# First projection of a two-block transformer kernel: its weights in quarters, x's second tile between them

## The reference

```
hn = rms_norm(h, attn_norm)
z = hn @ w_in                       # 1024 x 2048: q, k, v and u, 512 columns each
a_out = diff_attention(q, k, v, positions, q_norm, k_norm, lam_*, subln)
p_out = pool_mixer(u, w_pool, pool_scale)
h = h + concat(a_out, p_out) @ w_out
h = h + moe(rms_norm(h, ffn_norm), ...)     # 32 experts, each token in 4
```

## Time and profile before

| | us |
|---|---|
| median of 3 runs | 1755.04 (1754.52 to 1757.65) |
| profiled execution, its own time | 1755.88 |
| its span | 1753.7 |
| TensorE busy | 1677.8 (96%) |
| VectorE busy | 394.5 (22%) |
| ScalarE busy | 284.8 (16%) |
| HBM read | 654.14 MB, 374 GB/s over the span |

### The profile page before, as it was taken

How to read it: one execution, slowest core, us unless ns; L and a number is a source line. 1 busy time by engine, 2 the same in 40 slices (tenths; PEclk the granted TensorE clock), 3 DMA queues, 4 the chain that set the end, 5 groups by cost and what they waited for, 6 DMA issues and landing times.

```text
span 1753.7 us, 28543 instructions
## 1 busy us (share of the span) xinstructions
PE 1677.8 (96%) x11960; PEld 770.6 (44%) x11960; DVE 394.5 (22%) x943; ACT 284.8 (16%) x559; POOL 44.7 (3%) x115
## 2 busy tenths in 40 slices
PE   8999999999999999999999989999999999988887
PEld 4643333333333333333333334755545665654444
DVE  3543122121122112121121122453331111111111
ACT  3311111111121101100110012130112222111111
POOL 3140000000000000000000000000000000000000
PEclk9999999999999999999999999999999999999999
DMA  9769999999999999999999995533389999999997
GB/s 323 233 234 424 428 429 427 429 429 427 428 427 428 428 428 423 428 428 426 429 429 427 429 408 210 188 109 131 114 321 409 425 429 428 429 429 428 429 429 308
DMA packets 74394, 656.08 MB, mean 374 GB/s; under 512 B 13296, under 2 KB 16128, under 8 KB 36960
## 3 DMA queue, kind: packets, MB, share of 16 engines
q1 hardware_dynamic: 70880, 651.39, 89.7%
q0 software_dynamic: 688, 2.51, 0.4%
q10 hardware_dynamic: 2768, 1.31, 0.3%
HBM read 654.14 MB, written 1.05 MB: 374 GB/s over the span
## 4 chain that ended last, share of the span: by engine, by line
PE 76%; DMA 21%; DVE 1%; ACT 1%; issue 0%; SPq 0%; DVEq 0%
PE ps L1726 32%; DMA ring<-in_w_up_experts 11%; PE ps L1766 8%; PE ps L2132 6%; DMA ring<-in_w_up 6%; PE ps L2072 5%; PE ps L1711 4%; DMA scr<-in_w_up 4%; PE ps L1550 3%; PE ps L1817 3%; PE ps L1795 2%; PE ps L1720 2%; PE ps L1618 2%; PE ps L2310 2%; PE ps L1823 1%; PE ps L1781 1%
## 5 line engine op out<-in xcount | busy, mean ns | idle before, releaser
L1726 PE MATMUL ps<-ring,Z 128*64 128x512 f32 x2304 | 509.0, 595 | 11.9 <-DMA ring<-in_w_up 11.3
L1726 PEld LDWEIGHTS ps<-ring,Z 128*64 128x64 f32 x2304 | 165.5, 137 | 321.4 <-issue 291.4
L1766 PE MATMUL ps<-ring,Z 128*32 128x128 f32 x2752 | 164.8, 409 | 15.0 <-DMA ring<-in_w_up_experts 8.8
L1726 PE MATMUL ps<-scr,Z 128*64 128x512 f32 x768 | 170.3, 594 | 5.7 <-DMA scr<-in_w_up 5.7
L1766 PEld LDWEIGHTS ps<-ring,Z 128*32 128x32 f32 x2752 | 105.5, 127 | 70.4 <-DMA ring<-in_w_up_experts 13.3
L2132 PE MATMUL ps<-ring,both_x 128*128 128x512 f32 (+1 forms) x256 | 105.8, 567 | 0.0
L1726 PEld LDWEIGHTS ps<-scr,Z 128*64 128x64 f32 x768 | 54.8, 137 | 109.2 <-issue 95.2
L1711 PE MATMUL ps<-h,Z 128*32 128x256 f32 (+1 forms) x776 | 99.8, 468 | 0.5 <-DVE Z L1076 0.4
L1106 DVE TENSOR_SCALAR Z<-ps 128x512 f32<-128x512 f32 x32 | 22.1, 691 | 334.1 <-PE ps L1726 334.1
L677 ACT COPY Z<-ps 128x256 f32<-128x256 f32 (+1 forms) x63 | 30.1, 478 | 303.7 <-PE ps L1726 229.7
L668 ACT COPY Z<-ps 128x256 f32<-128x256 f32 x64 | 23.8, 372 | 312.8 <-PE ps L1774 312.8
(11 more groups left out here) (445 smaller groups left out, 1434.5 us busy)
## 6 DMA issues: line engine op xcount, KB each, us to landing
ring<-in_w_gate SPq DMA_DIRECT2D x48, 2048.0 KB, 24.6
ring<-in_w_up SPq DMA_DIRECT2D x48, 2048.0 KB, 27.2
ring<-in_w_down SPq DMA_DIRECT2D x48, 2048.0 KB, 29.4
ring<-in_w_gate_experts SPq DMA_DIRECT2D x21, 2048.0 KB, 32.4
ring<-in_w_up_experts SPq DMA_DIRECT2D x21, 2048.0 KB, 31.8
ring<-in_w_down_experts SPq DMA_DIRECT2D x21, 2048.0 KB, 31.3
scr<-in_w_down SPq DMA_DIRECT2D x16, 2048.0 KB, 28.7
scr<-in_w_gate SPq DMA_DIRECT2D x16, 2048.0 KB, 28.5
```

Of the source, the lines that this page charges most:

```text
L1726: last = pe.matmul(dst[CAP * j:CAP * (j + 1)], lhsT, rhs(j), start=start, stop=True, skip_group_check=True)
L1766: last = pe.matmul(bank(4)[CAP2 * t:CAP2 * (t + 1), P * s:P * (s + 1)], picked[:, chunk * CAP2:(chunk + 1) * CAP2], v[:, c, t:512:4], star ...
```

## The change

The first slot's weights come in four pieces of two chunks instead of two pieces of four. SyncE issues x tile 0, the gain, quarter 0, quarter 1, x tile 1, quarter 2, quarter 3 and then the slots as before. TensorE turns x tile 0, multiplies its first four chunks as the quarters land, turns tile 1, and multiplies the last four; the waits for `norm_xT` and for the weights come every two chunks. The turns fill the same banks in the same order. ScalarE, VectorE and GpSimd keep their code.

```diff
-        FRONT_PIECES = [2] + [1] * (SLOTS - 1)
+        FRONT_PIECES = [4] + [1] * (SLOTS - 1)
@@ SyncE
-            for a in range(TT):
+            def load_x(a):
                 sp.dma_start(h[:, a, :], w["x"][0, a * P:(a + 1) * P, :]).then_inc(sem(f"x_loaded{a}"), 16)
+
+            load_x(0)
             sp.dma_start(gcol[:, A_NORM, :], w["attn_norm"][0].rearrange("(p c) -> p c", p=P)).then_inc(sem("gain_loaded"), 16)
             for s, (src, c, n) in enumerate(front):
                 per = c // FRONT_PIECES[s]
                 for part in range(FRONT_PIECES[s]):
                     r = slice(part * per, (part + 1) * per)
-                    sp.dma_start(slot(s, c, n)[:, r, :], src[:, r, :]).then_inc(sem("first_half") if s == part == 0 else full[s], 16)
+                    sp.dma_start(slot(s, c, n)[:, r, :], src[:, r, :])\
+                        .then_inc(full[s] if part == FRONT_PIECES[s] - 1 else sem(f"first_quarter{part}"), 16)
+                    if s == 0 and part == 1:
+                        load_x(1)
@@ TensorE
-            for b in range(4):
-                pe.wait_ge(sem(f"x_loaded{b // 2}"), 16)
-                turn(bank(4 + b), h[:, b // 2, :], 4 * (b % 2), DC, 4, "norm_turned")
+
+            def turn_x(a):
+                pe.wait_ge(sem(f"x_loaded{a}"), 16)
+                for half in range(2):
+                    turn(bank(4 + 2 * a + half), h[:, a, :], 4 * half, DC, 4, "norm_turned")
 
             def project_in(j):
 
                 u, a = j // 2, j % 2
-                pe.wait_ge(sem("norm_xT"), 2 * a + 2)
-                pe.wait_ge(*((full[u], 16) if j else (sem("first_half"), 16)))
+                if j:
+                    pe.wait_ge(sem("norm_xT"), 2 * a + 2)
+                    pe.wait_ge(full[u], 16)
                 if j >= 2:
                     pe.wait_ge(sem("z_copied"), j - 1)
                 for c in range(DC):
                     if j == 0 and c == DC // 2:
-                        pe.wait_ge(full[0], 16)
+                        turn_x(1)
+                    if j == 0 and c % 2 == 0:
+                        pe.wait_ge(sem("norm_xT"), c // 4 + 1)
+                        pe.wait_ge(sem(f"first_quarter{c // 2}") if c < 6 else full[0], 16)
                     last = pe.matmul(bank(j % 2), xT[:, c, a * P:(a + 1) * P], slot(u, DC, 512)[:, c, :],
                                      start=c == 0, stop=c == DC - 1)
                 last.then_inc(sem("proj"), 1)
 
+            turn_x(0)
             for j in range(6):
                 project_in(j)
```

## The result

The changed kernel takes 1760.15 us (median of 11 runs, 1757.99 to 1765.95) against 1755.54 for the kernel before (11 runs, 1754.52 to 1757.65); the ratio is 1.0028, 95% interval 1.0019 to 1.0036. It is slower, by 4.6 us (0.28%; the interval leaves no change out). The profiled execution took 1759.94 with a span of 1757.8: 4.1 over the one of before.

What follows compares the result with a forecast made beforehand. TensorE was taken to bound the kernel (76% of the chain, DMA 21%). A wait of +3.2 and a slow restart of +1.8 gave +5.0 us, 1760.0 against 1755.04; 8-in-10 range 1755.6 to 1763.6.

Steps and rivals of the forecast that it cites:

- Landings: First slot and x tiles: quarter 0 at 6.2 to 7.5, tile 1 at 8.5 to 10.9, last quarter 13.4 or up to 1 later.
- turn_x(1): TensorE's turns of x tile 1 start at 12.6 us, bounds 10.9 and 13.9, after eight instructions taking 5.6.
- The gain: First projection ends at 16.9 instead of 19.6: 2.7 us saved, bounds 1.4 and 4.4; fourth ends at 37.5.
- The root: ScalarE's root, behind x tile 1's means, comes at 14.7 instead of 8.98: 5.7 us later, bounds 4.4 and 7.0.
- the whole shift passes: The small loads behind the root land later by its whole 5.7 us, `w_pool` at 38.9.
- The slack: In the kernel before, the third copy ends at 37.6, the fifth projection starts at 40.2: 2.6 us to spare.
- The wait: TensorE starts the fifth projection at 43.4 instead of 40.2, +3.2 us, after some 5.9 us idle.
- The restart: TensorE's slow clock after idling ahead of the fifth projection: +1.8 us, bounds 0 and 3.6.
- Nothing absorbs it: Behind the projections and through the expert stage, the shift of +5.0 us reaches the kernel's end whole.

Runs made afterwards that it cites:

- after_again: The changed kernel, unchanged, profiled once more; span 1762.7 us.
- before_again: The kernel before, unchanged, profiled once more; span 1754.6 us.
- kept_busy: The changed kernel with 22 bf16 products of zeros into a free bank ahead of the fifth projection; 1763.36 us, ratio 1.0055 to the kernel before.
- quarters_only: The kernel before with slot 0 in four quarters, both x tiles still in front; 1756.31 us, ratio 1.0000 to the kernel before.
- loads_late: The kernel before with five squares into unused space on ScalarE ahead of the small loads; 1756.14 us, ratio 1.0000.
- held_slots: The changed kernel with SyncE issuing slots 3 to 5 only when the nine small loads have landed; 1752.17 us, ratio 0.9977 to the kernel before.
- loads_early: The changed kernel with the small loads issued between the squares of the two x tiles; 1756.92 us, ratio 1.0006 to the kernel before.

## Why the prediction was right, point by point

The forecast was 1760.0, +5.0 us; measured 1760.15, +4.6. The chain is the one foretold, but several terms were off and cancelled in part. That the two times meet within 0.2 us is partly luck: the forecast was reckoned from a median of 1755.04, and over 11 runs it was 1755.54, which made up for the 0.4 by which the step was short.

- *Landings.* Quarter 0 at 6.1 (1.69+4.4), tile 1 at 9.8 (2.67+7.1), last quarter at 13.0 (3.67+9.3). Tile 1 was inside its bounds; quarter 0 was 0.1 before its earliest (6.2) and the last quarter 0.4 before (13.4). The 7.0 I took for the first product was 6.48.
- *`turn_x(1)`* at 11.58 instead of 12.6: it began 0.5 earlier, and eight instructions took 5.1 instead of 5.6, which is four at 0.86 and four at 0.43. (The granted clock prints 1.00 for all of this stretch and does not show the lower rate.)
- *The gain* at the end of the fourth projection was 40.2-36.66 = 3.5 instead of 2.7.
- *The root* at 13.87 instead of 14.7, 4.9 later where I had 5.7, in the bounds.
- *`w_pool`* was 18.9 us from issue to landing, as before (18.8), so from issue to landing "the whole shift passes" came out, at 37.6 instead of 38.9. From the root to the issue it did not quite: the ten issues ahead of `w_pool` took 4.9 us instead of 5.4, so 4.9 at the root became 4.4. But after_again has 21.2 and before_again 20.3: a single row stood for a quantity that scatters; `L923` starts at 33.22 in the earlier trace rows and at 34.55 in before_again. The slack there was 2.2 instead of 2.6, since TensorE was 1.0 later as well. That the first profile of the changed kernel drew 18.9 and not 21.2 is luck too.
- *The wait* at the fifth projection was +2.0 (42.20 against 40.2) where I had +3.2. This term was too large by 1.2, of which 0.8 came from the earlier root (13.87, not 14.7) and the rest from the shorter issues behind it.
- *The restart* cost 2.7 where I had 1.8: too small by 0.9. kept_busy shows the term by itself (16.46 to 13.97). before_again, with an idle of 2.63, paid 44.15-41.2 = 2.9 at its first projection, so the 1.8 was one draw as well. It was also read from another case: at 10.96 TensorE had not run at the full rate yet (16 turns in 3.33 us against 1.75), while at the fifth projection the clock fell from 1.00 and had to come back; that costs 1.9, 2.7 and 3.2 in quarters_only and the changed kernel's two profiles.
- *Nothing absorbs it.* The step held in every kernel without added products: turns from 50.4 to 58.7 go with spans from 1749.7 to 1757.8, and "rest" stays within 1698.6 to 1699.7. Only after_again, 1701.0, is outside, by the lower clock at 1058.

The sum of the profile is 4.6 at the turns and 4.1 at the end of the span; where the 0.5 between them went was not followed. What the prediction did not see: that the remedy lies on SyncE's queue, and that moving the loads to the front of ScalarE's would starve the second slot.

## What to carry to other kernels

When transfers or products are reordered at the start, follow every engine that waits for the moved piece to what it issues next: here a root that waited for x tile 1 held back eleven small loads, and the last of them had 2.6 us of slack before it held back a product that did not need it, through the order of two other engines. Small loads on a second queue shared the engines with the large ones packet for packet (356 and 358 from 18 to 21); to issue them earlier did not help here, but to hold back large loads that nobody needed yet did. Look also for a wait that asks for more loads than the work behind it reads. A landing read from one profile is a draw: a second profile of the unchanged kernel is worth taking when the slack is a few us.

## What the runs showed of the hardware

- The time from issue to landing of a 256 KB load of 512-byte rows behind ten other small ones, beside a full weights' queue, was 18.8 and 20.3 us in two profiles of one kernel, 18.9 and 21.2 in two of the other, up to 22.3 in a third (loads_late), and 11.6 in held_slots, where the weights were held back. The scatter is in its last packets: from 36 us on, 5 of 2224 were left in loads_late, 21 in the changed kernel and 87 in its second profile.
- ScalarE's queue issues transfers while an earlier instruction of ScalarE's stream still runs: five squares ahead of the loads delayed the last of them by 0.25 us. The other way round it waits: in loads_early the second square, behind the loads in the stream, began at 15.75, when the last issue (14.25, 1.45 us) was over.
- TensorE idle for 0.8 to 1.8 us ahead of the fifth projection: the next 32 instructions took 13.97; for 3.64, 15.67; for 5.54, 16.46; for 8.10, 16.90. In the four profiles of the first kind the granted clock stayed at 1.00; in the three others it fell to 0.50 at 40.4 to 40.5 (worked out from the 0.69, 0.73 and 0.75 that the 41st microsecond prints), in quarters_only 0.2 us after TensorE had begun again.
- 22 products in bf16 or five in float32 added to TensorE's stream at 36 us went with a stall of 5.18 or 3.04 us with no releaser at 1050 us and slower products after it. The slower products alone (8.72 us for 16 instead of 7.13, clock 0.50 from 1058 to 1060) also came in after_again, without added products or a stall. Open.
